# Level products of a recurrence in diagonal blocks, and another order of VectorE's work in each half step

## What is computed

```python
h = rmsnorm(x) * (1 + sc1) + sh1              # sc, sh, g: from silu(c) @ ada_w + ada_b, the modulation
q, ff, fb, iv, g, hy = split(h @ w_in)        # four heads of 128 keys and 128 values, and the Hyena part
log_f = log(lb + (1 - lb) * sigmoid(ff)); k = 1 - exp(log_f)      # fb likewise, for the backward scan
o, S = chunk_scan(silu(q) * 128 ** -0.5, k, iv, log_f, s0)        # in both directions, summed
o_hg = o * rsqrt(mean(o * o) + eps) * hg_norm_w * silu(g)
u = conv3(x1) * conv3(v); y_hy = conv3(x2) * (long_conv(u) + d * u)   # then normed
x = x + g1 * (concat(o_hg, y_hy) @ w_out)
x = x + g2 * convffn(rmsnorm(x) * (1 + sc2) + sh2)
```

## Time and profile before

| | |
|---|---|
| median of three runs | 908.77 us (907.77 to 908.89) |
| the profiled execution | 908.05 us, span 906.2 us |
| TensorE busy | 887.7 us, 98% of the span |
| VectorE busy | 714.4 us, 79% |
| ScalarE busy | 446.7 us, 49% |
| level products (L2263) | 280 records, 39.3 us busy, between 99.3 and 332 us |

### The profile page before, as it was taken

One profiled execution on the slowest core, in us unless ns is written; L12 is line 12 of the kernel. 1 busy time (PEld: TensorE's weight loads), 2 busy tenths in 40 slices (PEclk: granted clock), 3 DMA queues, 4 the chain that ended last, 5 costly groups with the idle time before them and its releaser, 6 DMA issues.

```text
span 906.2 us, 14128 instructions
## 1 busy us (share of the span) xinstructions
PE 887.7 (98%) x5384; PEld 788.9 (87%) x5384; DVE 714.4 (79%) x903; ACT 446.7 (49%) x718; POOL 38.7 (4%) x58
## 2 busy tenths in 40 slices
PE   7999999999999999999999999999999999999997
PEld 4469898998898898778889999999999999998885
DVE  5744764975966985599878899999999999988645
ACT  5835424324334333333566746565565656565443
POOL 2200000100000000101000000000000000000000
PEclk9999999999999999999999999999999999999999
DMA  8765143254044154323801233324313332345703
GB/s 282 261 195 197 60 151 121 50 163 142 28 163 146 45 184 162 94 70 59 244 1 47 76 131 103 109 95 131 99 64 133 116 107 81 131 164 194 261 0 117
DMA packets 39275, 112.76 MB, mean 124 GB/s; under 512 B 4471, under 2 KB 12663, under 8 KB 38568
## 3 DMA queue, kind: packets, MB, share of 16 engines
q1 hardware_dynamic: 33944, 93.58, 30.8%
q0 software_dynamic: 4800, 17.99, 6.6%
q10 hardware_dynamic: 464, 0.30, 0.1%
HBM read 101.48 MB, written 10.37 MB: 123 GB/s over the span
## 4 chain that ended last, share of the span: by engine, by line
PE 88%; DVE 5%; ACT 3%; DMA 2%; issue 2%; ACTq 0%; DVEq 0%; SPq 0%; POOLq 0%
PE ps L2042 19%; PE ps L2043 19%; PE ps L2044 19%; PE ps L2545 14%; PE ps L2263 3%; PE ps L2062 2%; PE ps L2123 2%; PE ps L2400 2%; PE ps L2445 1%; PE ps L2275 1%; DMA part<-in_rates 1%; DMA w<-in_hy_w 1%; PE ps L2070 1%; PE ps L2283 1%; DMA raw<-in_slots 1%
## 5 line engine op out<-in xcount | busy, mean ns | idle before, releaser
L2042 PE MATMUL ps<-h_hi,w_hi 128*128 128x320 f32 x588 | 186.3, 317 | 0.7 <-issue 0.7
L2044 PE MATMUL ps<-h_hi,w_lo 128*128 128x320 f32 x588 | 181.7, 309 | 0.0
L2043 PE MATMUL ps<-h_lo,w_hi 128*128 128x320 f32 x588 | 181.6, 309 | 0.0
L2042 PEld LDWEIGHTS ps<-h_hi,w_hi 128*128 128x128 f32 x588 | 110.7, 188 | 1.4 <-issue 1.4
L2043 PEld LDWEIGHTS ps<-h_lo,w_hi 128*128 128x128 f32 x588 | 110.6, 188 | 0.0
L2044 PEld LDWEIGHTS ps<-h_hi,w_lo 128*128 128x128 f32 x588 | 110.4, 188 | 0.0
L1905 DVE TENSOR_TENSOR w_lo<-raw,w_hi 128x1024 fp32r<-128x1024 f32 (+1 forms) x53 | 64.2, 1213 | 18.6 <-ACT w_hi L1253 17.6
L1253 ACT ACTIVATE w_hi<-raw 128x1024 fp32r<-128x1024 f32 (+1 forms) x53 | 55.5, 1048 | 31.1 <-PE ps L2044 31.0
L1411 DVE TENSOR_TENSOR w_lo<-raw,w_hi 128x1024 fp32r<-128x1024 f32 x42 | 51.1, 1225 | 6.8 <-ACT w_hi L917 5.8
L2042 PE MATMUL ps<-w_hi,h_hi 128*128 128x512 f32 x120 | 49.2, 410 | 0.3 <-issue 0.2
L1905 DVE TENSOR_TENSOR w_lo<-wsum,w_hi 128x1024 fp32r<-128x1024 f32 x38 | 46.4, 1222 | 1.0 <-ACT w_hi L1253 0.4
(11 more groups left out here) (341 smaller groups left out, 2120.5 us busy)
## 6 DMA issues: line engine op xcount, KB each, us to landing
raw<-in_slots SPq DMA_DIRECT2D x138, 512.0 KB, 4.8
acts<-actf POOLq DMA_DIRECT2D x22, 320.0 KB, 2.5
raw<-in_slots SPq DMA_DIRECT2D x24, 256.0 KB, 6.1
xf<-acts SPq DMA_DIRECT2D x12, 320.0 KB, 7.4
wsum<-acts SPq DMA_DIRECT2D x10, 320.0 KB, 7.8
xin<-in_x_sample SPq DMA_DIRECT2D x4, 512.0 KB, 11.3
grow<-gates POOLq DMA_DIRECT2D x2, 1024.0 KB, 11.5
x<-in_x_sample POOLq DMA_DIRECT2D x2, 1024.0 KB, 10.3
```

What stands on the lines that cost most here:

```text
L2042: mm(out, lhs[0], rhs[0], start=first, stop=False)
L2043: mm(out, lhs[0], rhs[1], start=False, stop=False)
L2044: return mm(out, lhs[1], rhs[0], start=False, stop=last)
```

## The change

Two edits. The first is in TensorE's levels: instead of one product of 128 keys by 128 queries for each chunk, only the diagonal blocks are made, of `wide` = 32 columns at levels 0 to 4 (four a chunk), 64 at level 5 (two), 128 at level 6 (one, as before). Each block writes its own partitions of the same bank, so the blocks of a chunk lie in different column groups of the array. What lies outside of the blocks is not written; no mask names it. `chunk` gets a `part` for this. The second is in VectorE's loop: the step, with `bound_gates` ahead of it, now comes right behind `pass_k`, and `split_lo`, `sum_groups` and `make_gain` come after the step.

```diff
--- before.py
+++ after.py
@@ -1661,6 +1661,11 @@
                 kind, i = TILES[n // 2]
                 if step_at(n):
                     pass_k(*step_at(n))
+                if n % 2 and kind in ("ff", "fb"):
+                    eng.wait_ge(sem("half_free"), n + 1)
+                    bound_gates(i, int(kind == "fb"))
+                if step_at(n):
+                    step(*step_at(n))
                 for unit in ahead(n):
                     split_lo(unit)
                 if n in ADA_SUM:
@@ -1668,11 +1673,6 @@
                     sum_groups(e)
                     if ADA_ORDER[e] == FINE[1]:
                         make_gain(1, "norm2")
-                if n % 2 and kind in ("ff", "fb"):
-                    eng.wait_ge(sem("half_free"), n + 1)
-                    bound_gates(i, int(kind == "fb"))
-                if step_at(n):
-                    step(*step_at(n))
                 if n % 2 and kind == "fb":
                     start_head(i)
                 if n == 2 * HEAD_TILES - 1:
@@ -2236,10 +2236,10 @@
                             last.then_inc(sem("unit_done"), 1)
                         after(p, i)
 
-            def chunk(h, j, c):
-
-                b = score_bank(h, j)
-                return ps[:, b, c * P:(c + 1) * P] if c < 4 else ps[:, b + 1, 0:P]
+            def chunk(h, j, c, part=slice(0, P)):
+
+                b, at = divmod(score_bank(h, j) * 4 + c, 4)
+                return ps[part, b, at * P + part.start:at * P + part.stop]
 
             def step(h, j):
                 if j == DIAG:
@@ -2259,9 +2259,13 @@
                         eng.wait_ge(sem("scores_taken"), j)
                     elif j >= 2:
                         eng.wait_ge(sem("scores_taken"), 8 * h + j - 1)
+
+                    wide = max(GROUP, 2 * s)
                     for c in range(NT):
-                        last = mm(chunk(h, j, c), kc[:, l % 2, c * P:(c + 1) * P],
-                                  ap(QQ, c * P, [(2 * s, P // (2 * s)), (T + s, 2), (1, s)]), start=True, stop=True)
+                        for g in range(P // wide):
+                            at = c * P + g * wide
+                            last = mm(chunk(h, j, c, slice(g * wide, (g + 1) * wide)), kc[:, l % 2, at:at + wide],
+                                      ap(QQ, at, [(2 * s, wide // (2 * s)), (T + s, 2), (1, s)]), start=True, stop=True)
                 elif j == KTURN:
                     eng.wait_ge(sem("k_next"), 8 * h + 8)
                     eng.wait_ge(sem("scores_taken"), 8 * h + 7)
```

## The result

| | before | changed |
|---|---|---|
| median | 908.75 us (907.77 to 908.89, 4 runs) | 919.6 us (918.37 to 919.98, 4 runs) |
| ratio | | 1.0122, 95% interval 1.0107 to 1.0138 |
| profiled execution | 908.05 us | 918.37 us |

The change makes the kernel 10.85 us slower. The forecast was 912.1 us with a range of 903 to 919: the sign was right, the size was three times too small, and the time lies 0.6 us beyond the range. The two profiled executions differ by 10.3 us; what follows accounts for this difference. The profiled execution of the changed kernel is the fastest of its four (mean grant of the clock 0.990); the other three have 0.986 to 0.989 and take 0.9 to 1.6 us longer.

A forecast was written before the change was run, and what follows sets the result against it. TensorE sets the end, but VectorE's run and the load chain behind w_lo hold it up to level 4. Heads at -3.5, +2.6, +1.6 and +2.6 sum to +3.3 us: 912.1 us as a median, range 903 to 919.

The forecast's parts named there:

- Part one: TensorE's block products: about 0.70 us for levels 1 to 4; 3.5 us of TensorE saved over a head.
- the sum: Heads 0 to 3 at -3.5, +2.6, +1.6 and +2.6 us, together +3.3 us, priced without a clock fall.
- Rival C: TensorE's levels: small matmuls don't overlap, a level stays at 1.12 us plus 0.32; +12 us, 920.8; chance 0.07.
- Part two: VectorE's order, step ahead of split_lo and sums: level 1 comes earlier, but two places delay w_lo and its load.
- (a): VectorE's NORM halves (n = 14, 26, 38): w_lo moves behind the RECIPROCAL, so all that follows comes 1.14 us later.
- (b): VectorE's halves with level 2: QQ, TU and scores, 2.12 us, now stand ahead of w_lo and delay the load.
- rival B: TensorE behind idles of 3 to 5 us, heads 1 to 3: clock falls to 1.2 GHz, 918 to 924; chance 0.13.
- the main case: Heads 1 to 3: the delayed load holds up level 4, TensorE idles 3 to 5 us; 912.1 us, chance 0.50.
- Rival A: Ahead of level 4: the delayed load isn't on the path; -9.0 us, 899.8; chance 0.20 with its partial form.
- Rival D: Whole stage: the terms cancel, by short loads (+0.4) or a larger gain in head 0; 907 to 910.5; chance 0.10.
- The signs to look for: Profile after: level 4 released by w_hi and a load, 3 to 5 us idle, level 1 without its 1 us idle.

The follow-up runs named there:

- the best kernel: Changed kernel with split_hi last on ScalarE in the halves with ada_turn and w_lo ahead of the step in the NORM halves: 895.93 us, ratio 0.9875.
- two blocks of 64 columns: Levels 0 to 4 in two 64-column blocks a chunk, against the best kernel's four of 32: 898.84 us, ratio 0.9902 to the kernel before.
- (b) undone: Changed kernel with w_lo ahead of the step again in the four halves with level 2 only: 908.56 us, ratio 1.0014 to the kernel before.

## Why the prediction was right in sign and wrong in size

**Part one: right.** The term of 0.35 + 0.32 us for a level held. Levels 4 and 5 of head 0, before and then changed, with the start of level 0 ahead:

```profile
122.11 1.28 PE L2263 MATMUL ps<-QQ,kc 128*128 128x128 f32 x10
...
126.74 1.27 PE L2263 MATMUL ps<-QQ,kc 128*128 128x128 f32 x10
```

```profile
98.73 0.63 PE L2267 MATMUL ps<-QQ,kc 128*32 128x32 f32 x40
...
118.46 0.56 PE L2267 MATMUL ps<-QQ,kc 128*32 128x32 f32 x40
...
122.66 0.80 PE L2267 MATMUL ps<-QQ,kc 128*64 128x64 f32 x20
```

From level 4 to level 5 it is 4.63 us before and 4.20 now: 0.43 saved, 0.42 predicted. At the full clock the 40 records start within 0.36 to 0.42 us (0.35 predicted), the 20 of 64 columns within 0.58. Head 0 gained 3.49 us for the 3.5 of the sum; head 1 of the best kernel has 3.3 us less work of TensorE than the head of the earlier trace rows. Rival C is out, and with it, as far as different column groups go, the floor of about 25 ns from start to start that the Trainium skill gives ("TensorE: Matmul & The Clock Gate", "Wait - 56ns, not 53.3ns?"): here it is about 10 ns.

**Part two, (a) and (b): right.** In head 1 TensorE idles from RECIPROCAL + 29.4 to + 34.7 (182.25 to 187.53) where + 29.2 to + 34.2 was forecast (186.4 and 191.4 less 157.16). Level 4 starts at + 35.7 for + 34.9; 0.4 of the 0.8 us is the longer load, and 0.5 the transposes at half clock. Terms at the full clock: +3.1, +2.1 and +3.1 for +2.6, +1.6 and +2.6. The 0.4 to 0.5 us each are the loads, 5.43, 3.64 and 4.76 us for the 5.07, 3.2 and 4.3 taken from the kernel before. They stood in the text as the uncertain size, but as one set of values.

**The clock: the step that failed.** The sum priced the work behind an idle that it had itself forecast, 5 us in head 1, at the full clock; measured, the half clock there cost 6.3 us in the three heads. The fall was put beside it as rival B with a chance of 0.13, as if it were another case; it is a consequence of the main case. The evidence at hand, idles of 1 us at a grant of 1.00, said nothing of 5 us. By B's own working the main case with the clock lost was 918 to 924; it was 919.6. The mechanism there was right (a half product and a level at half speed), its price of 2 to 4 us a head met in heads 2 and 3 (2.4 and 2.5) and too high in head 1 (1.4). Of the 7.5 us between the forecast +3.3 and the measured +10.85, 6.3 are the clock and 1.5 the longer loads; the earlier start of level 0 takes 0.8 off, and 0.5 is by how much the medians differ more than the profiled executions. The Trainium skill ("TensorE: Matmul & The Clock Gate", HAM oscillation) says that gaps between bursts of matmuls put the clock back; the windows above agree, 0.50 behind idles of 3.5 us and more. The runs add that idles of 1.8 to 2.5 us can do it too.

**Rival A** fell in all of its parts: the load was on the path in heads 1 to 3. By its own test, a w_lo at most 0.5 us later, it was out: w_lo of level 2's half starts at RECIPROCAL + 26.31 for + 23.04. The load left the path only when split_hi was moved, and then A's working came close (level 4 at RECIPROCAL + 29.7, 186.9 - 157.16, for 30.2 measured). **Rival D** fell with it.

**The signs to look for** appeared but for one: level 4 released by w_hi and a load, w_lo behind scores and in the NORM halves, 40 records of a level within 0.42 us; and of the signs for a wrong forecast the grant under 1.00 between 157 and 356 us. The one that failed is level 1. It was to stand no longer behind an idle of 1 us. It comes earlier, at RECIPROCAL + 13.36 for + 13.79, but TensorE, with its smaller level 0, is ready earlier still; and a second idle came ahead of level 3. Levels 1 and 3 of head 1 in the changed kernel:

```profile
166.23 0.55 PE L2267 MATMUL ps<-QQ,kc 128*32 128x32 f32 x40 [1.44 <-ACT kc L1045]
...
177.98 0.55 PE L2267 MATMUL ps<-QQ,kc 128*32 128x32 f32 x40 [1.40 <-ACT kc L1045]
```

The brackets name ScalarE's key gather, but VectorE's QQ ended later than it, 0.10 and 0.11 us ahead of the two levels. So the new order does bring VectorE's results forward, by less than the block products bring TensorE forward. Both idles lie where the prediction let TensorE's savings count for nothing, and no term depended on them.

## What to carry to other kernels

When a forecast opens an idle of TensorE, price the work behind it at both clock levels in the same sum; don't set the fall of the clock beside it as an unlikely case. Before an instruction is moved behind others, follow what its end releases through every queue: here a subtraction six halves ahead of its use gated a load, the load gated a rounding, and that stood ahead of a copy that TensorE needed at once. Where such a chain shows, move the waiting instruction behind the urgent ones on its own engine: that turned the same change from +10.9 into -6.8 us, and keeping w_lo in VectorE's idle at NORM made it -11.5.

## What the runs showed of the hardware

Idles of TensorE and the grant behind them, between 92 and 360 us of the twelve executions with a trace: at or behind idles of 3.46 to 5.28 us it fell to 0.50 in eight of eight, at 2.5 us in two of four, at 1.8 to 2.0 us in five of six, and at the 40 idles of 0.9 to 1.5 us never. Each stretch at half clock lasted 3.41 or 6.83 us, whatever the idle. An idle of 1.79 us took the clock in two cases of three and one of 2.55 us did not, and one of 1.90 us near the start of an execution (at 17.3 us, two blocks of 64 columns) did not either; so the length of one idle doesn't decide alone. What else does, the runs don't say. The same kernel also differs between executions: with the block products alone the clock fell twice in the traced one (mean grant 0.994) and by their mean grants of 0.998 to 0.999 not in the other three. Means of 0.996 in a few executions of the kernel before leave it open whether an idle of 1 us now and then takes the clock too.

Matmuls of 32 columns in four column groups start about 10 ns apart, weights included (40 within 0.37 us), in a kernel where a record of 128 columns takes 0.11 us.

The load of 512 KB that level 4 waits for took between 3.3 us (head 2, VectorE's order alone) and 6.03 us (head 1, (b) undone) from issue to landing. The runs don't show why.
